# RWKV solve: steps two and three put on the off-diagonal quarters of the array, X and G computed in both halves

## The chip, the cores and the metric

One core of one Trainium2 chip runs the whole program. The metric is the device time of one execution in microseconds. The kernel before was run three times: 4854.69 us in the median, 4831.49 to 4855.27. The profiled execution is a further one.

## The reference, cut to what matters

The program is one inference step of a two-layer hybrid encoder trunk. Each layer projects its input, runs three branches (RWKV-7 time mixing, latent attention, stick-breaking attention) and merges them. The change touches the RWKV branch alone, whose recurrence for each head of width 64 is:

```python
def step(S, inp):
    r_t, w_t, k_t, v_t, kk_t, a_t = inp
    sa = jnp.einsum('bhij,bhj->bhi', S, -kk_t)
    S = (S * w_t[:, :, None, :] + sa[..., :, None] * (kk_t * a_t)[..., None, :]
         + v_t[..., :, None] * k_t[..., None, :])
    return S, jnp.einsum('bhij,bhj->bhi', S, r_t)
```

The kernel doesn't step through time. For each 64-row chunk it solves a triangular system: the recurrence inside a chunk is (I - A) z = rhs, with A strictly triangular. A's 16-row diagonal blocks are inverted by a product of powers (1, 2, 4, 8), and the blocks below them, four block rows deep, are taken in by three repeated steps q = G + X q. The results are the solved rows Z and a transposed W, which a later stage uses.

## The kernel before, in words

`rwkv` calls `rwkv_solve` once per pair of heads: 2 layers x 4 pairs, 8 calls. A call works through 9 tiles of 128 rows (`NT` = 9): tiles 0 to 7 (`NPT` = 8) are the prompt, two chunks of 64 rows each; tile 8 holds the sample sequences, whose chunks are so short that they need no repeated steps. All data are float32.

Every product is a matmul of a 64x64 weight. With `HALVES` the two chunks of a tile lie in partitions 0 to 63 and 64 to 127; chunk r reads partitions of half r and writes PSUM partitions of half r, so it uses the diagonal quarter (r, r) of the 128x128 array. The off-diagonal quarters (r, 1-r) are used by `scores` (all four) and by `akv` in tiles 0 to 7.

The work of one tile i on TensorE, by the values of k in `turn` (L658 to L701) and the other helpers:

- `scores(i)`: L608, L611. `rows(i)`: four 128x128 transposes, L620 to L623. `akv(i)`: L634.
- k = 0: first squaring `power(i, 0)` (L642, L648).
- k = 1: `power(i, 1)` and `inverse(i, 0)` (L655). k = 2: `power(i, 2)` (L644) and `inverse(i, 1)`. k = 3: `inverse(i, 2)`.
- k = 4: X and G (L682, L684), called xg below.
- k = 5, 6, 7: the three steps q = G + X q (L696), called step 5, 6, 7 below, as in the code; k = 8: the transpose of W (L701).

The order is written out by hand, per engine, and each engine works strictly through its own list with semaphore waits. TensorE interleaves tile i's k = 0 to 4 with the older tile i-1's k = 5 to 8:

```python
for i in range(NT + 1):
    turn(i, 0); turn(i - 1, 5); scores(i + 1)
    turn(i, 1); turn(i - 1, 6); akv(i)
    turn(i, 2); turn(i - 1, 7); turn(i, 3)
    rows(i + 1); turn(i - 1, 8); turn(i, 4)
```

(The kernel has one call a line.) ScalarE evacuates PSUM: `power` copies (L738), `akv` (L746), `w` (L765), `x_and_g` (L755), `rows` (L727 to L730). VectorE adds and masks in this order, which the change leaves alone: `solved(i-1, 5)` (q, L848), `mask(i+1, 0)` (L792), `inverse(i, 0)` (L826), `solved(i-1, 6)` (q, L848), `inverse(i, 1)`, `mask(i+1, 2)`, `mask(i+1, 3)`, `solved(i-1, 7)` (Z and W rows, L842 and L844), `inverse(i, 2)`, `mask(i+1, 4)`, `mask(i+1, 1)` (L803).

Of the kernel before, what the change touches and what calls it, by code (L numbers as in the profile page):

```python
# [8 lines left out]
ALU = mybir.AluOpType  # L9
# [4 lines left out]
P = 128  # L14
# [525 lines left out]
def rwkv_solve(nc, S, A, l, ps, con, T_, h, nx):  # L540
# [4 lines left out]
    RW, BK, vT, WS = T_.RW[h % 2], T_.BK, T_.vT, T_.WS  # L545
    TM, SI, SS, Z = T_.TM, T_.SI, T_.SS, T_.Z
    names = ("rows_ready", "rows_copied", "scores_ready", "sc_masked", "masked", "akv_ready", "akv_copied", "power_ready", "power_copied",
             "e_ready", "e_added", "xg_ready", "xg_copied", "q_ready", "q_added", "w_rows", "w_ready", "w_copied", "scores_read", "first_loaded", "vec", "act_own")
    with S.stage(*names) as (block, sb, (rows_ready, rows_copied, scores_ready, sc_masked, masked, akv_ready, akv_copied, power_ready, power_copied,
                                         e_ready, e_added, xg_ready, xg_copied, q_ready, q_added, w_rows, w_ready, w_copied, scores_read, first_loaded, vec, act_own)):  # L550
# [46 lines left out]
        def _(pe):  # L597
# [36 lines left out]
                        last = mm(ps[HALVES[r], akv_bank(i, r), 64 * hh:64 * hh + 64], KA[i % 2][cc, hh, :], TM[cc, i, 2, hc], start=True, stop=True)  # L634
                last.then_inc(akv_ready, 1)

            def power(i, n):
                for hh in range(2):
                    for r, rc in enumerate(HALVES):
                        m, mt = PW[n][i % 2][rc, hh, 0:64], PW[n][i % 2][rc, hh, 64:P]  # L640
                        if n < 2:
                            mm(step(i, r, P * hh, 64), mt, m, start=True, stop=True)  # L642
                        else:
                            last = mm(step(i, r, 64 * hh, 64), mt, m, start=True, stop=True)  # L644
                    for r, rc in enumerate(HALVES):
                        m, mt = PW[n][i % 2][rc, hh, 0:64], PW[n][i % 2][rc, hh, 64:P]
                        if n < 2:
                            last = mm(step(i, r, P * hh + 64, 64), m, mt, start=True, stop=True)  # L648
                last.then_inc(power_ready, 1)

            def inverse(i, k):
                for hh in range(2):
# [5 lines left out]
            def turn(i, k):  # L658
                if not 0 <= i < NT:
                    return  # L660
                if k == 0:
                    pe.wait_ge(masked, i + 1)
                    if i >= 2:
                        pe.wait_ge(w_copied, i - 1)
                    power(i, 0)
                elif k <= 2:
                    pe.wait_ge(power_copied, 3 * i + k)
                    power(i, k)
                    if k == 2:
                        pe.wait_ge(e_added, 3 * i + 1)  # L670
                    inverse(i, k - 1)
                elif k == 3:
                    pe.wait_ge(power_copied, 3 * i + 3)
                    pe.wait_ge(e_added, 3 * i + 2)
                    inverse(i, 2)
                elif k == 4:
                    pe.wait_ge(e_added, 3 * i + 3)
                    pe.wait_ge(akv_copied, i + 1)
                    for hh in range(2):
                        if i < NPT:  # L680
                            for r, rc in enumerate(HALVES):
                                mm(step(i, r, 64 * hh, 64), LO[i % 2][rc, hh, :], ET[i % 2][rc, hh, :], start=True, stop=True)  # L682
                        for r, rc in enumerate(HALVES):
                            last = mm(step(i, r, P + P * hh, P), ET[i % 2][rc, hh, :], RH[i % 2][rc, hh, :], start=True, stop=True)  # L684
                    last.then_inc(xg_ready, 1)
                elif k <= 7:
                    if i == NPT:
                        return
                    if k == 5:
                        pe.wait_ge(xg_copied, i + 1)  # L690
                    else:
                        pe.wait_ge(q_added, 2 * i + k - 5)
                    for hh in range(2):
                        for r, rc in enumerate(HALVES):
                            rhs = G[i % 2][rc, hh, :] if k == 5 else Q[rc, hh, :]
                            last = mm(out(i, r, k, P * hh, P), X[i % 2][rc, hh, :], rhs, start=True, stop=True)  # L696
                    last.then_inc(q_ready, 1)
                else:
                    pe.wait_ge(w_rows, i + 1)
                    pe.wait_ge(xg_copied, i + 1)  # L700
                    nc.tensor.transpose(ps[:, step_bank(i), 0:P], WP[i % 2][:, :], ident).then_inc(w_ready, 1)  # L701

            scores(0)
            rows(0)
            for i in range(NT + 1):
                turn(i, 0)
                turn(i - 1, 5)
                scores(i + 1)
                turn(i, 1)
                turn(i - 1, 6)  # L710
                akv(i)
                turn(i, 2)
                turn(i - 1, 7)
                turn(i, 3)
                rows(i + 1)
                turn(i - 1, 8)
                turn(i, 4)

        @block.scalar
        def _(act):  # L720
            copy = nc.scalar.activation

            def rows(i):
                if not 0 <= i < NT:
                    return
                act.wait_ge(rows_ready, i + 1)
                copy(RH[i % 2][:, :, 0:64], by_head(ps[:, 3, 0:P]), ACT.Copy)  # L727
                if i < NPT:
                    copy(TM[64:P, i, 3, :], ps[64:P, 3, 3 * P:4 * P], ACT.Copy)
                copy(TM[:, i, 0:3, :].rearrange("p q n -> p (q n)"), ps[:, 3, P:4 * P], ACT.Copy).then_inc(rows_copied, 1)  # L730

            def power(i, n):
                if not 0 <= i < NT:
                    return
                act.wait_ge(power_ready, 3 * i + n + 1)
                dst, w = (PW[n + 1][0], 2 * P) if n < 2 else (P8, P)
                for rc, bank in read_parts(i):
                    last = copy(dst[rc, :, :].rearrange("p h n -> p (h n)"), ps[rc, bank, 0:w], ACT.Copy)  # L738
                last.then_inc(power_copied, 1)

            def akv(i):
                if not 0 <= i < NT:
                    return
                act.wait_ge(akv_ready, i + 1)
                for rc, bank in akv_parts(i):
                    last = copy(RH[i % 2][rc, :, 64:P], by_head(ps[rc, bank, 0:P]), ACT.Copy)  # L746
                last.then_inc(akv_copied, 1)

            def x_and_g(i):
# [6 lines left out]
                last.then_inc(xg_copied, 1)  # L756

            def w(i):
                if not 0 <= i < NT:
                    return  # L760
                act.wait_ge(w_ready, i + 1)
                if i == NPT:
                    copy(WS[:, :], ps[:, step_bank(i), 0:P], ACT.Copy).then_inc(w_copied, 1)
                else:
                    copy(RW[:, i, 2:6:3, :], ps[:, step_bank(i), 0:P].rearrange("p (s n) -> p s n", s=2), ACT.Copy).then_inc(w_copied, 1)  # L765

            rows(0)
            for i in range(NT + 1):
                power(i, 0)
                power(i, 1)  # L770
                akv(i)
                power(i, 2)
                w(i - 1)
                x_and_g(i)
                rows(i + 1)

        @block.vector
        def _(dve):
# [50 lines left out]
            def solved(i, k):  # L829
# [3 lines left out]
                if i == NPT:  # L833
# [1923 lines left out]
```

## Time and profile before

| | |
|---|---|
| median of three runs | 4854.69 us |
| the profiled execution | 4857.2 us |
| its span, first to last instruction | 4855.6 us |
| mean granted TensorE clock | 0.96 |
| TensorE busy in the span | 4409.6 us (91%) |
| VectorE, ScalarE, GpSimd busy | 2218.3, 1625.0, 731.2 us |
| TensorE on L655, L642, L648, L696, L684 | 89.9, 82.4, 78.9, 80.6 + 41.9, 51.5 us |

"Busy" of TensorE counts a matmul from its start to its modelled end, and matmuls overlap, so a busy TensorE is not one that could take no more. The last row gives the solve's main groups. A timeline of one tile's turn says more about this stage than the shares do; such rows are given below. In them "xN" is the number of instruction records in the row (every float32 matmul here leaves two), the first number is the start in us from the span's start, and the second is the time from the first start to the last end.

### The profile page before, as it was taken

To read this page: it belongs to the slowest core of one execution; us is meant where nothing else is said; L and a number is where in the kernel's file an instruction comes from. 1 tells how busy PE (TensorE), PEld (TensorE's weight loads), DVE (VectorE), ACT (ScalarE), POOL (GpSimd) and SP (SyncE) were. 2 spreads that over 40 slices of the span, in tenths; PEclk is the share of its full clock that TensorE was granted. 3 is DMA by queue.
4 is the path that set the end of the run, shared out by engine and by line. 5 is a ranking of instruction groups with operands and counts; after the bars stand their busy time and mean duration, and the time that the engine had idled before them with its cause. 6 is when DMAs were issued, how large, how long until landed. Compare 5 with 4: busy or idle time off the path is not lost. (4 is left out here: it accounts for less than half of the span.)

```text
span 4855.6 us, 75921 instructions
## 1 busy us (share of the span) xinstructions
PE 4409.6 (91%) x29552; PEld 3049.7 (63%) x29552; DVE 2218.3 (46%) x4656; ACT 1625.0 (33%) x3862; POOL 731.2 (15%) x940
## 2 busy tenths in 40 slices
PE   5989897989889989999968999879898899899999
PEld 2656655657666667777436566656576666677774
DVE  2455655245524463434224555542455344535342
ACT  3324333345533342112033233333455334421110
POOL 0010010000001005543000100100000100155430
PEclk8999999999999999999989999989999999999999
DMA  5110110210021113232240101111100211223222
GB/s 223 27 17 26 25 28 24 74 51 20 16 73 63 56 46 107 94 105 74 75 185 22 33 10 25 28 40 58 51 20 16 82 54 56 73 84 110 88 78 69
DMA packets 152509, 292.71 MB, mean 60 GB/s; under 512 B 51769, under 2 KB 77625, under 8 KB 146818
## 3 DMA queue, kind: packets, MB, share of 16 engines
q1 hardware_dynamic: 152034, 283.07, 18.2%
q8 instruction: 238, 3.90, 0.3%
q10 hardware_dynamic: 112, 4.72, 0.3%
q14 instruction: 125, 1.02, 0.1%
HBM read 240.40 MB, written 52.06 MB: 60 GB/s over the span
## 5 line engine op out<-in xcount | busy, mean ns | idle before, releaser
L1041 PE MATMUL banks<-hT,w_piece 128*128 128x384 f32 x1536 | 550.8, 500 | 10.4 <-ACT raw L1145 10.2
L1041 PEld LDWEIGHTS banks<-hT,w_piece 128*128 128x128 f32 x1536 | 282.2, 195 | 181.3 <-issue 16.3
L2226 PE MATMUL banks<-hT,w_piece 128*128 128x384 f32 x1056 | 354.1, 489 | 1.5 <-ACT sb_gate_raw L2336 1.5
L2226 PEld LDWEIGHTS banks<-hT,w_piece 128*128 128x128 f32 x1056 | 196.1, 190 | 141.4 <-issue 16.6
L2577 PE MATMUL banks<-hT,mergedT 128*128 128x512 f32 x576 | 247.5, 592 | 0.0
L1992 DVE SCALAR_TENSOR_TENSOR keysT<-banks,gains,rstd 64x128 f32<-64x128 f32 (+1 forms) x272 | 112.1, 412 | 250.4 <-ACT rstd L1906 247.9
L2623 DVE TENSOR_TENSOR gate_quarters<-gate_kept,banks 128x288 f32<-128x288 f32 x144 | 65.4, 454 | 306.3 <-PE banks L2518 301.3
L2586 ACT ACTIVATE gate_kept<-banks 128x288 f32<-128x288 f32 x144 | 59.0, 410 | 434.8 <-PE banks L2518 434.8
L2577 PEld LDWEIGHTS banks<-hT,mergedT 128*128 128x128 f32 x576 | 109.4, 190 | 137.0 <-issue 136.8
L2398 DVE TENSOR_TENSOR_SCAN left<-pass,zero 128x384 f32<-128x384 f32 (+7 forms) x144 | 190.5, 1323 | 5.0
L2623 DVE TENSOR_TENSOR branch_quarters<-branch_kept,banks 128x288 f32<-128x288 f32 x144 | 65.4, 454 | 267.2 <-PE banks L2518 267.1
L2395 DVE TENSOR_TENSOR pass<-pass,constants 128x128 f32<-128x128 f32 x128 | 40.8, 319 | 312.1 <-ACT take L2347 309.5
L1002 POOL TENSOR_TENSOR state_decayed<-state,decay_of_chunk 128x128 f32<-128x128 f32 x120 | 85.9, 716 | 586.9 <-DVE state L1274 586.9
L1824 PE MATMUL banks<-keysT,queriesT 96*128 96x512 f32 (+3 forms) x384 | 151.9, 504 | 8.7 <-DVE queriesT L1992 8.7
L2518 PE MATMUL banks<-hT,w_gate_ahead 128*128 128x288 f32 x576 | 153.0, 417 | 7.4 <-PEq L132 7.4
L2518 PE MATMUL banks<-y_branch,w_branch 128*128 128x288 f32 x576 | 155.4, 406 | 0.0
L2518 PE MATMUL banks<-hT,w_gate 128*128 128x288 f32 x576 | 147.5, 406 | 0.0
L2518 PEld LDWEIGHTS banks<-hT,w_gate_ahead 128*128 128x128 f32 x576 | 112.3, 196 | 40.6 <-issue 8.8
L1922 ACT ACTIVATE exponentials<-banks,maximum 128x384 f32<-128x384 f32 (+4 forms) x144 | 104.1, 723 | 92.1 <-DVE maximum L2005 91.1
L2223 PE MATMUL banks<-w_piece,hT 128*128 128x128 f32 x1152 | 132.7, 276 | 0.0
L1933 ACT ACTIVATE exponentialsT<-banks 128x512 f32<-128x512 f32 (+3 forms) x208 | 94.9, 488 | 110.1 <-PE banks L1836 109.3
L2223 PEld LDWEIGHTS banks<-w_piece,hT 128*128 128x128 f32 x1152 | 130.2, 192 | 1.0
(393 smaller groups left out, 9476.2 us busy)
## 6 DMA issues: line engine op xcount, KB each, us to landing
w_piece<-in_w_cols SPq DMA_DIRECT2D x66, 512.0 KB, 4.4
w_ada<-in_w_ada SPq DMA_DIRECT2D x24, 1024.0 KB, 9.6
w_gate_ahead<-in_w_cols SPq DMA_DIRECT2D x48, 512.0 KB, 4.2
w_branch<-in_w_br SPq DMA_DIRECT2D x96, 256.0 KB, 2.8
w_gate<-in_w_cols SPq DMA_DIRECT2D x48, 512.0 KB, 4.2
y_branch<-y_gated SPq DMA_DIRECT2D x12, 1152.0 KB, 8.5
sb_cached_keysT<-in_sbkT SPq DMA_DIRECT2D x8, 1024.0 KB, 7.3
sb_cached_values<-in_sbv SPq DMA_DIRECT2D x8, 1024.0 KB, 5.2
```

The lines of the kernel that those rows point to most:

```text
L1002: G.tensor_tensor(SD[:, :], ST[:, :], R.pend[h % 2][:, n + 1:n + 2].broadcast_to([P, P]), ALU.mult).then_inc(sd_made, 1)
L1041: last = mm(dst, w[0 if kind in ("k", "v") else 1][:, k, :], hT[:, k, c], start=(k == 0), stop=(k == KD - 1))
L1824: last = mm(ps[:, b0 + a // 512, 0:e - a], Q[hh][:, P * i:P * i + P], K[hh][:, a:e], start=True, stop=True)
L1922: do(E[u % 3][:, 0:width(u)], sbank(u)[:, 0:width(u)], ACT.Exp, bias=mx[:, u:u + 1], scale=scale, accum_out=rsum[:, u:u + 1]).then_inc(exp ...
L1933: do(ET[:, s % 4, units[u][3], 0:cnt, :].rearrange("p q n -> p (q n)"), ps[:, ring_bank(("t", u, g)), 0:P * cnt], Copy).then_inc(ring_free, 1)
L1992: ins = V.scalar_tensor_tensor(to[hh][0:64, c], ps[hc, bank[n], at], par[hc, gain:gain + 1], rs[x % 2][hc, at], ALU.mult, ALU.mult)
L2223: last = mm(ps[:, bank[n], P * q:P * q + P], hT[:, k, P * i:P * i + P], w_of[wn][:, k, :], start=(k == 0), stop=(k == KD - 1))
L2226: last = mm(ps[:, bank[n], 0:TG], w_of[wn][:, k, :], hT[:, k, TG * g:TG * g + TG], start=(k == 0), stop=(k == KD - 1))
L2398: own(V.tensor_tensor_scan(mine[:, 0:n][:, ::-1], G[k][:, 0:n][:, ::-1], zero[:, 0:1].broadcast_to([P, n]), 1.0, ALU.mult, ALU.add))
L2518: ins = mm(ps[:, bank, 0:TQ], w[:, k, :], b[:, k, :], start=(first and k == 0), stop=(k == half - 1), skip_group_check=True)
L2577: last = mm(ps[:, banks[j % 4], :], M[:, k, P * i:P * i + P], w_half(n)[:, k, :], start=(k == 0), stop=(k == KD - 1))
L2623: own(V.tensor_tensor(dst, src, ps[:, bank, 0:TQ], ALU.add), added)
```

## The change

Steps 6 and 7 of tile i-1 run on the off-diagonal quarters, interleaved instruction by instruction with powers 2 and 4 of tile i. For that X and G are also computed with their halves swapped, into PSUM bank 2, and copied by a new ScalarE copy `swapped` to a new tile. Step 6 takes X from its own half and leaves its result in the other; its sum uses the swapped G; step 7 takes the swapped X and comes back. ScalarE's `rows(i + 1)` is moved ahead of `w` and `x_and_g`. VectorE's order stays.

```diff
+        SW = sb("x_and_g_swapped", [P, 3 * P])
...
+        XS, GS = SW[:, 0:P].rearrange("p (h n) -> p h n", h=2), SW[:, P:3 * P].rearrange("p (h n) -> p h n", h=2)
...
-            def power(i, n):
-                for hh in range(2):
-                    for r, rc in enumerate(HALVES):
...
+            def square(i, n, hh, r, transposed):
+                m, mt = PW[n][i % 2][HALVES[r], hh, 0:64], PW[n][i % 2][HALVES[r], hh, 64:P]
+                if transposed:
+                    return mm(step(i, r, P * hh + 64, 64), m, mt, start=True, stop=True)
+                return mm(step(i, r, (P if n < 2 else 64) * hh, 64), mt, m, start=True, stop=True)
+
+            def across(i, k, hh, r):
+                if not 0 <= i < NPT:
+                    return None
+                lhsT, rhs = (X[i % 2], Q) if k == 6 else (XS, Q)
+                return mm(out(i, 1 - r, k, P * hh, P), lhsT[HALVES[r], hh, :], rhs[HALVES[r], hh, :], start=True, stop=True)
...
+            def powers_and_step(i, n):
+                stepped = 0 <= i - 1 < NPT
+                if stepped:
+                    pe.wait_ge(q_added, 2 * (i - 1) + n)
+                    if n == 2:
+                        pe.wait_ge(swap_copied, i)
+                if i < NT:
+                    pe.wait_ge(power_copied, 3 * i + n)
+                for hh in range(2):
+                    for r in range(2):
+                        if i < NT:
+                            power = square(i, n, hh, r, 0)
+                        turned = across(i - 1, n + 5, hh, r)
+                    if i < NT and n < 2:
+                        for r in range(2):
+                            power = square(i, n, hh, r, 1)
+                if stepped:
+                    turned.then_inc(q_ready, 1)
+                if i < NT:
+                    power.then_inc(power_ready, 1)
+                    if n == 2:
                         pe.wait_ge(e_added, 3 * i + 1)
-                    inverse(i, k - 1)
...
+                    inverse(i, n - 1)
...
+            def x_and_g(i):
+                if i >= NT:
+                    return
+                pe.wait_ge(e_added, 3 * i + 3)
+                pe.wait_ge(akv_copied, i + 1)
+                if 1 <= i < NPT:
+                    pe.wait_ge(swap_copied, i)
+                for hh in range(2):
+                    for r, rc in enumerate(HALVES):
                         if i < NPT:
...
+                            mm(step(i, r, 64 * hh, 64), LO[i % 2][rc, hh, :], ET[i % 2][rc, hh, :], start=True, stop=True)
+                            mm(ps[HALVES[1 - r], 2, 64 * hh:64 * hh + 64], LO[i % 2][rc, hh, :], ET[i % 2][rc, hh, :], start=True, stop=True)
+                    for r, rc in enumerate(HALVES):
+                        last = mm(step(i, r, P + P * hh, P), ET[i % 2][rc, hh, :], RH[i % 2][rc, hh, :], start=True, stop=True)
+                        if i < NPT:
+                            last = mm(ps[HALVES[1 - r], 2, P + P * hh:2 * P + P * hh], ET[i % 2][rc, hh, :], RH[i % 2][rc, hh, :], start=True, stop=True)
+                last.then_inc(xg_ready, 1)
...
             for i in range(NT + 1):
-                turn(i, 0)
-                turn(i - 1, 5)
+                first_power(i)
+                first_step(i - 1)
                 scores(i + 1)
-                turn(i, 1)
-                turn(i - 1, 6)
+                powers_and_step(i, 1)
                 akv(i)
-                turn(i, 2)
-                turn(i - 1, 7)
-                turn(i, 3)
+                powers_and_step(i, 2)
+                last_inverse(i)
                 rows(i + 1)
-                turn(i - 1, 8)
-                turn(i, 4)
+                turn_w(i - 1)
+                x_and_g(i)
...
+            def swapped(i):
+                if not 0 <= i < NPT:
+                    return
+                act.wait_ge(xg_ready, i + 1)
+                if i >= 1:
+                    act.wait_ge(q_ready, 3 * i)
+                    act.wait_ge(q_added, 2 * i)
+                copy(SW[:, :], ps[:, 2, 0:3 * P], ACT.Copy).then_inc(swap_copied, 1)
+
...
                 power(i, 0)
+                swapped(i - 1)
                 power(i, 1)
                 akv(i)
                 power(i, 2)
+                rows(i + 1)
                 w(i - 1)
                 x_and_g(i)
-                rows(i + 1)
...
                 dve.wait_ge(q_ready, 3 * i + k - 4)
+                if k == 6:
+                    dve.wait_ge(swap_copied, i + 1)
...
-                        ins = V.tensor_tensor(Q[rc, :, :], g[rc, :, :], by_head(q), ALU.add)
+                        ins = V.tensor_tensor(Q[rc, :, :], (g if k == 5 else GS)[rc, :, :], by_head(q), ALU.add)
```

`first_power`, `first_step`, `last_inverse` and `turn_w` hold the same matmuls and waits as `turn` with k = 0, 5, 3 and 8.

## Rows read from the trace of the kernel before

**Rows 1.** Windows: length, then busy us of each engine, clock, DMA.

```profile
195.05:245.05 50.00, 46.93 (x1087) 40.48 (x1082) 32.61 (x106) 22.36 (x72) 0.00 (x0) 1.00 0.03 9
3652.20:3655.60 3.40, 1.82 (x14) 1.59 (x14) 2.30 (x9) 1.89 (x6) 0.00 (x0) 1.00 0.16 58
```

**Rows 2.** Timeline of TensorE's matmuls in one turn: start, length, instruction.

```profile
214.36 0.54 PE L696 MATMUL banks<-x_and_g 64*64 64x128 f32 x5
...
214.80 0.55 PE L608 MATMUL banks<-a_r_and_w,k_and_b 64*64 64x128 f32 x12
...
215.59 0.33 PE L642 MATMUL banks<-power 64*64 64x64 f32 x4
...
216.10 0.40 PE L655 MATMUL banks<-inverseT,power 64*64 64x64 f32 x8
216.34 0.28 PE L696 MATMUL banks<-q,x_and_g 64*64 64x128 f32 x2
216.35 0.27 PE L634 MATMUL banks<-bk_and_vu_rows,scores_ka 64*64 64x64 f32 x2
...
216.67 0.28 PE L696 MATMUL banks<-q,x_and_g 64*64 64x128 f32 x2
216.78 0.42 PE L644 MATMUL banks<-power 64*64 64x64 f32 x8
217.04 0.40 PE L655 MATMUL banks<-inverseT,power 64*64 64x64 f32 x8
217.54 0.65 PE L696 MATMUL banks<-q,x_and_g 64*64 64x128 f32 x8
218.02 0.41 PE L655 MATMUL banks<-inverseT,power 64*64 64x64 f32 x8
...
218.75 0.27 PE L623 MATMUL banks<-constants,k_and_b 128*128 128x128 f32 x1
...
219.13 0.33 PE L682 MATMUL banks<-inverseT,off_diagonal 64*64 64x64 f32 x4
```

**Rows 3.** Timeline of VectorE in the same turn.

```profile
215.06 0.42 DVE L848 TENSOR_TENSOR q<-x_and_g,banks 128x256 f32<-128x256 f32 x1 [0.69 <-PE banks L696]
...
216.62 0.29 DVE L826 TENSOR_TENSOR inverseT<-inverseT,banks 128x128 f32<-128x128 f32 x1 [0.63 <-PE banks L655]
217.06 0.42 DVE L848 TENSOR_TENSOR q<-x_and_g,banks 128x256 f32<-128x256 f32 x1 [0.15 <-PE banks L696]
217.55 0.29 DVE L826 TENSOR_TENSOR inverseT<-inverseT,banks 128x128 f32<-128x128 f32 x1
...
218.79 0.29 DVE L826 TENSOR_TENSOR inverseT<-inverseT,banks 128x128 f32<-128x128 f32 x1
```

**Rows 4.** Timeline of ScalarE in the same turn and to the next.

```profile
213.82 0.49 ACT L755 ACTIVATE x_and_g<-banks 128x384 f32<-128x384 f32 x1 [0.76 <-PE banks L684]
214.21 0.27 ACT L727 ACTIVATE rhs<-banks 128x128 f32<-128x128 f32 x1
214.49 0.27 ACT L729 ACTIVATE bk_and_vu_rows<-banks 64x128 f32<-64x128 f32 x1
...
215.16 0.38 ACT L738 ACTIVATE power<-banks 128x256 f32<-128x256 f32 x1
...
220.07 0.49 ACT L755 ACTIVATE x_and_g<-banks 128x384 f32<-128x384 f32 x1 [0.61 <-PE banks L684]
```

**Rows 5.** Timeline of TensorE in a call's last turn, `akv` on the diagonal.

```profile
240.90 0.60 PE L696 MATMUL banks<-q,x_and_g 64*64 64x128 f32 x8
241.33 0.40 PE L634 MATMUL banks<-bk_and_vu_rows,scores_ka 64*64 64x64 f32 x8
```

**Rows 6.** Timeline of ScalarE, start and end of that last turn.

```profile
238.78 0.49 ACT L755 ACTIVATE x_and_g<-banks 128x384 f32<-128x384 f32 x1 [0.59 <-PE banks L684]
...
244.43 0.38 ACT L755 ACTIVATE x_and_g<-banks 128x256 f32<-128x256 f32 x1 [0.38 <-PE banks L684]
```

More of the change, by code:

```diff
@@ L656, in inverse, with first_power @@
                 last.then_inc(e_ready, 1)
-            def turn(i, k):
-                if not 0 <= i < NT:
+            def first_power(i):
+                if i >= NT:
                     return
[L661 to L669, printed above, removed]
-                        pe.wait_ge(e_added, 3 * i + 1)
-                    inverse(i, k - 1)
[L672 to L679, printed above, removed]
-                        if i < NPT:
[L681 to L701, printed above, removed]
@@ new lines, in first_power, with first_step @@
+                pe.wait_ge(masked, i + 1)
+                if i >= 2:
+                    pe.wait_ge(w_copied, i - 1)
+                for hh in range(2):
+                    for transposed in range(2):
+                        for r in range(2):
+                            last = square(i, 0, hh, r, transposed)
+                last.then_inc(power_ready, 1)
+            def first_step(i):
+                if not 0 <= i < NPT:
+                    return
+                pe.wait_ge(xg_copied, i + 1)
+                for hh in range(2):
+                    for r, rc in enumerate(HALVES):
+                        last = mm(out(i, r, 5, P * hh, P), X[i % 2][rc, hh, :], G[i % 2][rc, hh, :], start=True, stop=True)
+                last.then_inc(q_ready, 1)
@@ new lines, in powers_and_step @@
+            def powers_and_step(i, n):
[6 more added lines that the diff above has]
+                    pe.wait_ge(power_copied, 3 * i + n)
+                for hh in range(2):
+                    for r in range(2):
[3 more added lines that the diff above has]
+                    if i < NT and n < 2:
+                        for r in range(2):
+                            power = square(i, n, hh, r, 1)
[4 more added lines that the diff above has]
+                    if n == 2:
+                        pe.wait_ge(e_added, 3 * i + 1)
+                    inverse(i, n - 1)
@@ new lines, in last_inverse @@
+            def last_inverse(i):
+                if i >= NT:
+                    return
+                pe.wait_ge(power_copied, 3 * i + 3)
+                pe.wait_ge(e_added, 3 * i + 2)
+                inverse(i, 2)
+            def x_and_g(i):
+                if i >= NT:
+                    return
+                pe.wait_ge(e_added, 3 * i + 3)
+                pe.wait_ge(akv_copied, i + 1)
+                if 1 <= i < NPT:
+                    pe.wait_ge(swap_copied, i)
+                for hh in range(2):
+                    for r, rc in enumerate(HALVES):
+                        if i < NPT:
+                            mm(step(i, r, 64 * hh, 64), LO[i % 2][rc, hh, :], ET[i % 2][rc, hh, :], start=True, stop=True)
+                            mm(ps[HALVES[1 - r], 2, 64 * hh:64 * hh + 64], LO[i % 2][rc, hh, :], ET[i % 2][rc, hh, :], start=True, stop=True)
+                    for r, rc in enumerate(HALVES):
+                        last = mm(step(i, r, P + P * hh, P), ET[i % 2][rc, hh, :], RH[i % 2][rc, hh, :], start=True, stop=True)
+                        if i < NPT:
+                            last = mm(ps[HALVES[1 - r], 2, P + P * hh:2 * P + P * hh], ET[i % 2][rc, hh, :], RH[i % 2][rc, hh, :], start=True, stop=True)
+                last.then_inc(xg_ready, 1)
@@ L703, in _, with turn_w @@
+            def turn_w(i):
+                if i < 0:
+                    return
+                pe.wait_ge(w_rows, i + 1)
+                pe.wait_ge(xg_copied, i + 1)
+                nc.tensor.transpose(ps[:, step_bank(i), 0:P], WP[i % 2][:, :], ident).then_inc(w_ready, 1)
             scores(0)
@@ L756, in x_and_g @@
                 last.then_inc(xg_copied, 1)
+            def swapped(i):
+                if not 0 <= i < NPT:
+                    return
+                act.wait_ge(xg_ready, i + 1)
[3 more added lines that the diff above has]
+                copy(SW[:, :], ps[:, 2, 0:3 * P], ACT.Copy).then_inc(swap_copied, 1)
             def w(i):
```

14 lines of the change are left out of this document (2 added, 12 removed).

## The prediction

> **What bounds the solve now.** I read the granted clock and busy time of a stretch first, then the timelines of the three working engines through one turn, from one xg copy on ScalarE to the next. Over 50 us of the first call TensorE is busy 46.93 us at the full clock of 2.4 GHz [rows 1]. That looks like a TensorE bound, and it isn't one: that time counts each matmul to its modelled end, and those ends overlap. The turn has to be followed from release to release. It is 6.25 us long (213.82 to 220.07) [rows 4]; the last turn of a call is 5.65 us (238.78 to 244.43) [rows 6]. There are 8 turns in each of 8 calls, 64 in all: 64 x 6.2 = about 400 us of 4857 that the change can touch.
>
> I count from the xg copy, called a0 (213.82). Step 5 starts at a0+0.54 and its sum q on VectorE runs from a0+1.24 to a0+1.66 [rows 2, 3]. ScalarE, after xg, first does the `rows` copies and only then the power copy (a0+1.34 to 1.72), and that releases power 1 at a0+1.77 (215.59) [rows 2, 4]. From there: inverse 0 at +0.51 after power 1, its sum on VectorE at +1.03; the sum of step 6 at +1.47; power 2 at +1.19, inverse 1 at +1.45; step 7 at +1.95, 0.06 after the end of step 6's sum [rows 2, 3]. VectorE works in its written order, so the sum of inverse 1 (217.55) waits for step 6's sum (end 217.48), though its own matmuls, 217.04 + 0.40, were done. The reader should see in these rows that **two chains share VectorE**: the powers with the inverse, and the steps. From the sum of inverse 1 the end of the turn is fixed: 1.24 us of VectorE work (two masks, Z, W rows) to the sum of inverse 2 at 218.79, 0.34 to xg at 219.13, 0.94 to the next xg copy at 220.07 [rows 2 to 4]. So what matters is when the sum of inverse 1 starts: a0+3.73 now. 3.73 + 1.24 + 0.34 + 0.94 = 6.25.
>
> **The change, part by part.**
>
> Do the quarters work side by side? `akv` is issued after step 6. In ordinary tiles it is on the off-diagonal quarters and its first matmuls start at 216.35, with step 6's first at 216.34, while step 6's last start at 216.67 [rows 2]. In a call's last tile `akv` is on the diagonal and starts at 241.33, 0.43 after step 6's 240.90 [rows 5]. So a step costs 0.43 on its own quarters and nothing on the others. Scores use all four quarters: 12 records of 128 columns take 0.55 us, 0.27 of it the last one's length, so they start 25 ns apart; the 8 of step 7 alone take 0.65, with 0.28 for the last, 53 ns apart [rows 2]. I take the off-diagonal work as free of array time.
>
> Block one, power 1 with step 6. The block now waits for the sum of step 5, ending a0+1.66, plus 0.06: it starts at **a0+1.72** instead of a0+1.77. Behind the waiting block stand inverse 0 and `akv`. The power copy is no longer behind `rows` (the move) and is ready earlier, at about a0+0.39 + 0.38 + 0.05 = a0+0.82, so the new wait is the later one. Gain 0.05. Power 1 keeps its diagonal quarters 0.51 us, in which step 6 (0.43) runs beside it.
>
> VectorE's turn comes next, and here the gain is lost. Inverse 0 is still issued behind power 1, so its sum starts at +1.03 and ends at +1.32. The sum of step 6 is written behind it on VectorE: it starts, with 0.04 between dependent sums, at +1.36 although its matmuls were done at about 0.7, and ends at +1.78. Before it started at +1.47. Moving step 6 0.75 us forward has brought its sum forward by only 0.11.
>
> Block two, power 2 with step 7, now waits for that sum: it starts at 1.72 + 1.78 + 0.06 = **a0+3.56**. Step 7 is 0.16 earlier than before (a0+3.72), but power 2, which used to start at a0+2.96 as soon as its copy was there, is 0.60 later, and inverse 1 stands behind it. Inverse 1 at +0.26 (its distance behind power 2 now), its sum 0.51 after (217.04 to 217.55, of which 0.40 + 0.11 are its own latency, as for inverse 0: 216.10 to 216.62): a0 + 3.56 + 0.77 = **a0+4.33**, where it was a0+3.73. Step 7's matmuls end 0.65 after their start, a0+4.21, so Z and W rows, behind two masks, are not late. Inverse 2 needs the sum's end, a0+4.62 + 0.06 = 4.68, and its own sum could go at 5.20; VectorE is free at 4.33 + 1.24 = 5.57. So the tail of 1.24 + 0.34 + 0.94 stays and each turn is **+0.60 us**.
>
> In the last turn the next tile's masks and `rows` are absent, so the tail is shorter, but the same wait for step 6's sum stands ahead of inverse 1. I take 0.60 there too, an estimate for 8 turns of the 64; between 0.3 and 0.7 it moves the sum by 2 us at most.
>
> X and G twice: 8 more matmuls a tile, on the other quarters beside the old ones. At the rate of scores, 25 ns a record, its 16 records of 128 columns take 0.40 us and the 16 of 64 columns, at half of that, 0.20: 0.60, where the 8 and 8 of now at 53 and 27 take 0.64. So nothing; if they didn't overlap at all, 0.64 a turn. I take 0, since scores are the nearest row.
>
> The new copy `swapped`, 0.49 (the length of its twin L755 [rows 4]), comes after the power copy, a0+0.8 to 1.3. ScalarE's next is the copy of power 1 at about a0+2.45. It is covered; without that cover it would be 0.4 (its pitch) a turn. Its data are wanted at a0+3.1 first. `rows` on ScalarE moved before `w` and xg: the transposes are ready 1.00 after the start of inverse 2 (218.02 to 218.75 + 0.27 [rows 2]), at a0+5.68, plus 0.04; three copies have a pitch of 0.95 (214.21 to 215.16), `w` 0.28 at most (214.21 to 214.49) [rows 4], so xg can be copied at a0+6.95 against 6.85 ready. Between 0 and 0.10; I take 0.05, in 56 turns (the last turn of a call has no `rows`).
>
> Sum: 64 x 0.60 = 38.4, 56 x 0.05 = 2.8, together **+41 us**. On the profiled execution (4857.2) that is 4898.4; the median is 2.5 below it, so I forecast **4896 us**.
>
> A rule weighed against the rows: the Trainium skill, "TensorE: Matmul & The Clock Gate", section "Part 3: Packing small matmuls — row/col tiling", says that MATMULs keep program order in start and end and only weight loads are pulled ahead. By that rule `akv` could not start at 216.35, before step 6's remaining starts up to 216.67 [rows 2]; the trace disagrees. What such an order would give is the second rival.
>
> **The rivals.**
>
> *Faster, because TensorE is what binds.* Then what leaves the diagonal quarters counts: step 6, 0.44 (216.34 to 216.78), and step 7, 0.48 (217.54 to 218.02) [rows 2], 0.92 x 64 = 59 us, 4796. The busy share [rows 1] speaks for it. It decides the time only if power 2 starts no later than now, that is if the sum of step 6 ended by about a0+2.9; VectorE's order puts it at 3.50. Chance 4%.
>
> *Slower by more: starts in program order.* If a step's third and fourth matmul must start before what is issued behind them, power 2 and inverse 1 are stretched by the step: inverse 1 at +0.43 to 0.46 after block two instead of 0.26. +0.2 x 64 = 13 us, 4909. For it: power and step are now interleaved one by one. Against it: [rows 2, 5]. Chance 20%.
>
> *No change that shows.* If the sum of step 6 were not held behind inverse 0 (say its sum comes out when its own matmuls end, a0+2.45 to 2.87), block two would start at a0+2.93 and inverse 1's sum at a0+3.70, a parity: 4855. VectorE's list speaks against it. Together with partial covers that eat half of the sum: chance 10%.
>
> *The change doesn't do what it says:* off-diagonal work not free. xg twice is +0.6 and the steps in the powers' way another 0.4: 64 x 1.0 = 64 us more, 4960. Scores and `akv` [rows 2, 5] speak against it. Chance 4%.
>
> *The clock falls within the solve,* since TensorE now idles about 0.9 us before block two in each turn. A stretch with 1.82 us busy of 3.40 kept the full clock [rows 1], and the solve keeps about three quarters busy. Chance 2%; at 1.2 GHz the 400 us would grow by a quarter or more, over 4950.
>
> **How the numbers follow.** The forecast has 60%, with its own range of 4884 to 4908 (ScalarE 0 to 0.10 a turn, 0.1 us either way in the turn). I widen to the in-order case above and to part-covers and a differently placed clock fall between stages (the three runs are 24 us apart) below: 4872 to 4916. A difference of 0.5%, 24 us, is about what a measurement of this kernel can tell from none. Slower by more than that: forecast, in-order case, the last two, less the forecast's low tail: 0.85. Within: 0.11. Faster: 0.04.
>
> **What would show it.** The turn between xg copies at 6.85 to 6.95; TensorE idle about 0.9 us ahead of power 2 (L644's successor), released by the sum q on VectorE, not by the power copy; the sum of step 6 starting within 0.05 of the end of inverse 0's; `swapped` never a releaser; `akv`, power 2 and inverse 1 starting while the step beside them still has starts to come. A turn under 6.4, or power 2 starting about 1.2 after power 1, would prove me wrong; a turn of 7.05 with inverse 1 0.45 behind power 2 would show the order rule; a longer xg to first power would show quarters that collide.

## The result and the profile after

The changed kernel takes 4928.35 us in the median (4925.7 to 4934.3, four runs) against 4853.91 us: a ratio of 1.0159, 95% interval 1.0138 to 1.0181. It is slower by 74 us. The forecast was 4896 us, 41 us slower, with a range up to 4916: the side was right, the size was not. The traces are 77.1 us apart (4932.7 against 4855.6). From the first to the last xg copy of a call passes 49.4 to 49.7 us before and 57.8 to 58.8 after, 68.8 us over the eight calls. The other 8.3 us lie outside the solves.

The page of the changed kernel: line, engine, instruction, count, then busy us, mean ns, and TensorE's idle time ahead of these instructions with what ended it.

```profile
L643 PE MATMUL banks<-power 64*64 64x64 f32 x1728 | 121.3, 238 | 77.9 <-DVE q L890 57.0
L655 PE MATMUL banks<-inverseT,power 64*64 64x64 f32 x1728 | 92.9, 224 | 47.3 <-DVE inverseT L866 47.3
```

L643 is the squaring in the three powers, L655 the matmuls of the inverse. TensorE now idles 57.0 us before it for the sum q, 0.89 in each of 64 turns, as forecast (0.9). Before, TensorE's idle time ahead of L655 was 4.8 us in all. The windows of the changed kernel (as in [rows 1]) say the same: over the same 50 us TensorE is busy 37.86 us, not 46.93, and the clock isn't full throughout.

```profile
195.05:245.05 50.00, 37.86 (x1051) 32.62 (x1043) 28.70 (x95) 20.89 (x66) 0.00 (x0) 0.93 0.01 3
```

Now one usual turn of the changed kernel, to be held against [rows 2 to 4]. ScalarE first:

```profile
222.31 0.49 ACT L760 ACTIVATE bk_and_vu_rows<-banks 128x384 f32<-128x384 f32 x1
222.70 0.27 ACT L804 ACTIVATE a_r_and_w<-banks 128x128 f32<-128x128 f32 x1
222.86 0.50 ACT L785 ACTIVATE x_and_g<-banks 128x384 f32<-128x384 f32 x1
223.84 0.38 ACT L768 ACTIVATE power<-banks 128x256 f32<-128x256 f32 x1 [0.48 <-PE banks L642]
224.12 0.49 ACT L795 ACTIVATE x_and_g_swapped<-banks 128x384 f32<-128x384 f32 x1
225.54 0.38 ACT L768 ACTIVATE power<-banks 128x256 f32<-128x256 f32 x1 [0.93 <-PE banks L642]
...
227.29 0.28 ACT L768 ACTIVATE power<-banks 128x128 f32<-128x128 f32 x1 [1.20 <-PE banks L643]
...
230.12 0.50 ACT L785 ACTIVATE x_and_g<-banks 128x384 f32<-128x384 f32 x1
```

VectorE in the same turn:

```profile
224.28 0.42 DVE L890 TENSOR_TENSOR q<-x_and_g,banks 128x256 f32<-128x256 f32 x1 [0.98 <-PE banks L676]
...
225.78 0.29 DVE L866 TENSOR_TENSOR inverseT<-inverseT,banks 128x128 f32<-128x128 f32 x1 [0.60 <-PE banks L655]
226.10 0.42 DVE L890 TENSOR_TENSOR q<-x_and_g_swapped,banks 128x256 f32<-128x256 f32 x1
227.49 0.29 DVE L866 TENSOR_TENSOR inverseT<-inverseT,banks 128x128 f32<-128x128 f32 x1 [0.97 <-PE banks L655]
...
228.73 0.29 DVE L866 TENSOR_TENSOR inverseT<-inverseT,banks 128x128 f32<-128x128 f32 x1
```

TensorE in the same turn:

```profile
221.81 0.27 PE L720 MATMUL banks<-inverseT,off_diagonal 64*64 64x64 f32 x1
...
223.12 0.33 PE L643 MATMUL banks<-power 64*64 64x64 f32 x4 [0.41 <-ACT a_r_and_w L804]
...
223.60 0.49 PE L676 MATMUL banks<-x_and_g 64*64 64x128 f32 x5
...
224.75 0.27 PE L643 MATMUL banks<-power 64*64 64x64 f32 x1
...
226.58 0.27 PE L643 MATMUL banks<-power 64*64 64x64 f32 x1 [0.85 <-DVE q L890]
...
226.80 0.23 PE L643 MATMUL banks<-power 64*64 64x64 f32 x2
...
226.86 0.22 PE L655 MATMUL banks<-inverseT,power 64*64 64x64 f32 x1
...
226.97 0.28 PE L649 MATMUL banks<-q,x_and_g_swapped 64*64 64x128 f32 x2
226.98 0.29 PE L655 MATMUL banks<-inverseT,power 64*64 64x64 f32 x4
227.93 0.45 PE L655 MATMUL banks<-inverseT,power 64*64 64x64 f32 x8 [0.66 <-DVE inverseT L866]
...
229.07 0.27 PE L720 MATMUL banks<-inverseT,off_diagonal 64*64 64x64 f32 x1
```

The reader is to see three things. Power 2 (226.58) starts on the end of step 6's sum (226.10 + 0.42), which started when inverse 0's sum (225.78 + 0.29) was done; the power's own copy had ended at 225.54 + 0.38, 0.60 before the sum did. The first power of this turn (223.12) waited for W's copy (222.70 + 0.27), 1.31 after xg's start at 221.81, where it was 0.72. And inverse 1's sum (227.49) comes 0.22 after its matmuls' modelled end (226.98 + 0.29), where it was 0.11. The turn in four pieces, cut as the prediction cuts it:

| us | xg copy to power 1 | to inverse 1's sum | to inverse 2's sum | to next xg copy | turn |
|---|---|---|---|---|---|
| before | 1.77 | 1.96 | 1.24 | 1.28 | 6.25 |
| forecast | 1.72 | 2.61 | 1.24 | 1.33 | 6.90 |
| after | 1.89 | 2.74 | 1.24 | 1.39 | 7.26 |

### The profile page after: what moved, and what is told of

Same layout as the page of the kernel before. It is cut to its first block and busy times, and to the rows that moved or that the text cites. A ratio compares the mean times of both kernels' runs of the same rounds, so it can differ in the third digit from the quotient of the medians.

```text
span 4932.7 us, 78217 instructions
## 1 busy us (share of the span) xinstructions
PE 4391.1 (89%) x30576; PEld 3019.8 (61%) x30576; DVE 2213.9 (45%) x4656; ACT 1652.4 (33%) x3926; POOL 731.8 (15%) x940
## 5 line engine op out<-in xcount | busy, mean ns | idle before, releaser
L643 PE MATMUL banks<-power 64*64 64x64 f32 x1728 | 121.3, 238 | 77.9 <-DVE q L890 57.0
L643 PEld LDWEIGHTS banks<-power 64*64 64x64 f32 x1728 | 90.4, 142 | 108.8 <-DVE q L890 67.7
L768 ACT ACTIVATE power<-banks 128x256 f32<-128x256 f32 (+1 forms) x216 | 75.2, 348 | 184.1 <-PE banks L642 105.5
L655 PE MATMUL banks<-inverseT,power 64*64 64x64 f32 x1728 | 92.9, 224 | 47.3 <-DVE inverseT L866 47.3
```

The costliest lines, as they stand in the source:

```text
L643: return mm(step(i, r, (P if n < 2 else 64) * hh, 64), mt, m, start=True, stop=True)
```

## The experiments

Each ran beside the kernel before on the same chip; the ratio to it is given with its 95% interval. The chip was not the same for all experiments, so where times of different experiments are compared, the ratios or the distances to the kernel before are taken. The pieces of a turn are read in the third call's third turn.

**Rows copies back in their place (e1).**

```diff
                 power(i, 2)
-                rows(i + 1)
                 w(i - 1)
                 x_and_g(i)
+                rows(i + 1)
```

> Changed kernel, with ScalarE's rows(i+1) back behind w and x_and_g; nothing else. Theory: the move put the copy of W behind three rows copies, and the first power of the next tile waits for that copy (215.86 in the changed kernel, 1.16 after xg's start, where it was 0.72), and step 5 stands behind it on TensorE. Undone, xg to its copy is 0.94 again instead of up to 1.12 and xg copy to power 1 is 1.77 instead of 1.83: the usual turn 7.26 becomes 7.0 to 7.05, in 56 turns 12 to 14 us, about 4915. Rival, the prediction's term for the move (0.05 a turn): 3 us, 4925. Second rival, the move also helps by letting the power copy go early: no change or slower.

Measured: 4926.66 us, 1.0138 (1.0121 to 1.0155). The usual turn is 7.15. ScalarE and TensorE of this kernel:

```profile
573.57 0.49 ACT L785 ACTIVATE x_and_g<-banks 128x384 f32<-128x384 f32 x1 [0.65 <-PE banks L725]
...
574.91 0.38 ACT L768 ACTIVATE power<-banks 128x256 f32<-128x256 f32 x1
```

```profile
574.11 0.54 PE L676 MATMUL banks<-x_and_g 64*64 64x128 f32 x5 [0.15 <-ACT x_and_g L785]
...
575.43 0.24 PE L643 MATMUL banks<-power 64*64 64x64 f32 x1
```

Both things that I wanted undone are undone: step 5 starts 0.54 after the xg copy, not 0.74, and xg is copied 0.08 sooner. But power 1 starts at +1.86, hardly before the +1.89 of the changed kernel: the power copy is behind `rows` again and ends at +1.72. So the move has a gain (the power copy is early) and a price (W's copy, and with it the next tile's first power, step 5 and its sum, are late), and they nearly cancel. My expectation took the price alone as theory and left the gain to a rival, though both count: 0.11 a turn, not 0.21 to 0.26. In the time it can't be told from nothing.

**No wait in front of the power (e2).**

```diff
-                if stepped:
-                    pe.wait_ge(q_added, 2 * (i - 1) + n)
-                    if n == 2:
-                        pe.wait_ge(swap_copied, i)
+                if stepped and n == 1:
+                    pe.wait_ge(q_added, 2 * (i - 1) + n)
...
+                if stepped and n == 2:
+                    pe.wait_ge(q_added, 2 * (i - 1) + n)
+                    pe.wait_ge(swap_copied, i)
+                    for hh in range(2):
+                        for r in range(2):
+                            turned = across(i - 1, n + 5, hh, r)
+                    turned.then_inc(q_ready, 1)
```

> Changed kernel, with power 4's squaring and inverse 1 issued as soon as their own inputs are there; step 7 stays on the off-diagonal quarters but is issued behind them, with the wait for step 6's sum in front of it alone. Theory: the loss is that wait in front of the power. The power starts 1.19 after power 1 again instead of 1.82, inverse 1's sum starts 1.97 after power 1 instead of 2.74; the turn 7.26 becomes about 6.5, 48 us over 64 turns, about 4880. Rival (the loss is in computing X and G twice, in quarters that collide or in the clock): 4920 or more.

Measured: 4874.07 us, 1.0034 (1.0021 to 1.0047); turn 6.54. TensorE of this kernel:

```profile
565.55 0.27 PE L643 MATMUL banks<-power 64*64 64x64 f32 x1
...
566.77 0.45 PE L643 MATMUL banks<-power 64*64 64x64 f32 x8 [0.24 <-ACT power L774]
567.05 0.40 PE L655 MATMUL banks<-inverseT,power 64*64 64x64 f32 x8
567.38 0.65 PE L649 MATMUL banks<-q,x_and_g_swapped 64*64 64x128 f32 x8
```

Power 2 is released by its own copy again, 1.22 after power 1, and step 7 follows on its own quarters beside inverse 1. This one edit takes the ratio from 1.0159 to 1.0034, about four fifths of the loss: 15 us over the kernel before are left of 74. The theory holds, in mechanism and size; X and G are still computed twice. But the edit does two things: it takes the wait away from the power, and it takes step 7's matmuls out from among the power's. The next experiment does the second alone and has a turn of 7.14; the wait by itself is the difference to it, 7.14 - 6.54 = 0.60 a turn, the forecast's own term (37 us by the medians, of the same chip).

**Same waits, step 7 issued last (e3).** The waits stay at the head of block two; the four squarings and the four matmuls of inverse 1 are issued ahead of step 7's four instead of among them.

```diff
-                        turned = across(i - 1, n + 5, hh, r)
+                        if n == 1:
+                            turned = across(i - 1, n + 5, hh, r)
...
                     inverse(i, n - 1)
+                if stepped and n == 2:
+                    for hh in range(2):
+                        for r in range(2):
+                            turned = across(i - 1, n + 5, hh, r)
+                    turned.then_inc(q_ready, 1)
```

> Changed kernel, block two with the same waits at its head, but the four matmuls of the power and the four of inverse 1 are issued first and step 7 behind them. Theory (a matmul group's signal waits for what was issued before it, although starts overlap): inverse 1's sum, now 0.92 after the block's start, comes at 0.77 as in the kernel before; the turn 7.26 becomes 7.11, 9 to 10 us, about 4918; the power copy comes 0.55 after the block's start instead of 0.71. Rival (step 7 slows the neighbours because both read the same partitions): sum stays at 0.9, no change.

Measured: 4911.18 us, 1.0106 (1.0087 to 1.0124); turn 7.14. TensorE, and then ScalarE and VectorE behind it:

```profile
578.37 0.45 PE L643 MATMUL banks<-power 64*64 64x64 f32 x8 [0.85 <-DVE q L896]
578.65 0.22 PE L655 MATMUL banks<-inverseT,power 64*64 64x64 f32 x2
```

```profile
578.86 0.28 ACT L774 ACTIVATE power<-banks 128x128 f32<-128x128 f32 x1 [0.99 <-PE banks L643]
```

```profile
579.16 0.29 DVE L872 TENSOR_TENSOR inverseT<-inverseT,banks 128x128 f32<-128x128 f32 x1 [0.85 <-PE banks L655]
```

The power copy comes 0.49 after the block's start and inverse 1's sum 0.79, against 0.71 and 0.91 in the changed kernel (226.58 to 227.29 and 227.49). The turn is shorter by the same 0.12, so that is what step 7 in between cost. It is 8 us over 64 turns; the solves of this trace are 14.6 us shorter than the changed kernel's (450.3 against 464.9), and the clock falls of the changed kernel, described below, are absent from them. The rest of the difference in time lies outside the solves. In the changed kernel the power's last matmuls (the row at 226.80, two records) have their modelled end at 227.03, and ScalarE is released only at 227.29, with the end of step 7 (226.97 + 0.28 = 227.25). The trace also records when the semaphores were raised: the power's at 227.26, step 7's at 227.31 and inverse 1's at 227.40, which is the order in which they were issued, and in e3, with step 7 issued last, the power's at 578.84, inverse 1's at 579.07 and step 7's at 579.34. Starts overtake one another across quarters, signals do not. That speaks against the expectation's rival too, a step that slows its neighbours by reading the same partitions: the power's last matmul starts about 0.23 behind its first in the changed kernel and in e3 alike, so the matmuls were not slowed, their signal was held.

The trace of the kernel before had the sign of it. There `akv` is issued behind step 6; its matmuls end by the model at 216.79, and its copy starts only at 217.08, after step 6's end (216.67 + 0.28 = 216.95 in [rows 2]):

```profile
216.57 0.22 PE L634 MATMUL banks<-bk_and_vu_rows,scores_ka 64*64 64x64 f32 x2
```

```profile
217.08 0.28 ACT L746 ACTIVATE rhs<-banks 128x128 f32<-128x128 f32 x1 [0.38 <-PE banks L634]
```

The Trainium skill's rule in "TensorE: Matmul & The Clock Gate", section "Part 3: Packing small matmuls — row/col tiling", that matmuls keep order in start and end, is by these rows wrong for the starts; for the ends the signals agree with it (the ends in the rows are modelled and settle nothing).

**VectorE takes step 6's sum first (e4).**

```diff
-                inverse(i, 0)
                 solved(i - 1, 6)
+                inverse(i, 0)
                 inverse(i, 1)
```

> Changed kernel, with VectorE taking step 6's sum before inverse 0's; nothing else. Theory (step 6's matmuls are done early, at 0.7 after power 1, and only VectorE's order holds its sum to 1.35): the sum starts at about 0.75, block two starts 1.23 after power 1 instead of 1.82, inverse 1's sum 2.2 after power 1 instead of 2.74: turn 7.26 becomes about 6.7, 35 us, about 4893. Rival (step 6 isn't early, the off-diagonal matmuls are late themselves): the sum starts at 1.2 or later and the turn stays above 7.1.

Measured: 4886.69 us, 1.0063 (1.0045 to 1.0081); turn 6.74. VectorE of this kernel, whose power 1 starts at 557.00:

```profile
557.78 0.42 DVE L890 TENSOR_TENSOR q<-x_and_g_swapped,banks 128x256 f32<-128x256 f32 x1 [0.34 <-PE banks L649]
558.24 0.29 DVE L866 TENSOR_TENSOR inverseT<-inverseT,banks 128x128 f32<-128x128 f32 x1
559.23 0.29 DVE L866 TENSOR_TENSOR inverseT<-inverseT,banks 128x128 f32<-128x128 f32 x1 [0.70 <-PE banks L655]
```

The sum starts 0.78 after power 1 instead of 1.35: the off-diagonal matmuls were done, VectorE's order held the sum. Exchanging two lines takes the ratio to 1.0063, more than half of the loss: 28 us over the kernel before are left of 74.

**X and G twice in the kernel before (e7).** The 8 extra matmuls and the copy `swapped` are those of the change's diff; nothing reads the copy, and steps 5 to 7 stay as before.

> Kernel before, with X and G computed a second time on the off-diagonal quarters into bank 2 and copied by ScalarE behind the first power copy, as in the changed kernel; the copy is read by nothing. It prices the doubling by itself. Theory: the quarters work side by side and the copy falls into ScalarE's idle time; xg start to its copy is 0.97 instead of 0.94, the turn 6.25 becomes 6.25 to 6.35, under 6 us, 4855 to 4865. Rival (the doubling holds a good part of the loss): 0.3 to 0.64 a turn, 4875 to 4900.

Measured: 4860.79 us, 1.0007 (0.9995 to 1.0020); turn 6.28. The doubling costs 0.03 a turn, 2 us over the 64 turns; the time itself can't be told from that of the kernel before.

**Both undone (e9)**: e2 and e1 together.

> Changed kernel with both undone, the wait for step 6's sum in front of the power and the move of ScalarE's rows; steps on the off-diagonal quarters, step 6 interleaved with power 2 and the doubling stay. It closes the account. Theory: from the turn of the kernel with the first undone (6.54) the move gives 0.1 back, as it did when undone alone (7.26 to 7.15): 6.43, and what is left over the kernel before (6.25) is the doubling's 0.03 and power 1 about 0.1 later behind its wait for step 5's sum; some 4864 to 4872. Rival (the two undone overlap, one hides the other): 6.5 or more, or 6.3 or less.

Measured: 4862.63 us, 1.0013 (1.0002 to 1.0025); turn 6.43, as expected, and the time just under the 4864 to 4872 expected. Its pieces are 1.86, 2.02, 1.24 and 1.31. Against the kernel before, 0.03 is the doubling, 0.09 power 1 and 0.06 the longer way to inverse 1's sum. Why power 1 starts 0.14 after the end of the power copy (0.05 before), with the sum of step 5 already there, I didn't find.

**Rows copies behind the first power copy, in the kernel before (e5).** If the power copy's place matters, it can be had without the change:

```diff
                 power(i, 0)
+                if i:
+                    rows(i)
                 power(i, 1)
                 akv(i)
                 power(i, 2)
                 w(i - 1)
                 x_and_g(i)
-                rows(i + 1)
```

> Kernel before, with ScalarE's rows copies of tile i behind the first power copy of tile i, where they stand neither before the power copy nor before W and xg; TensorE and VectorE as before. Theory: power 1 starts when scores leave the array, about 1.6 after the xg copy instead of 1.77; turn 6.25 becomes about 6.1, 8 to 11 us less, about 4845. Rival (TensorE's queue is full): no change.

Measured: 4829.95 us, 0.9948 (0.9931 to 0.9965), **faster than both kernels**; turn 6.01. TensorE and ScalarE of this kernel:

```profile
543.22 0.38 PE L611 MATMUL banks<-k_and_b,a_r_and_w 64*64 64x64 f32 x5
543.43 0.28 PE L642 MATMUL banks<-power 64*64 64x64 f32 x4
```

```profile
541.85 0.49 ACT L755 ACTIVATE x_and_g<-banks 128x384 f32<-128x384 f32 x1 [0.61 <-PE banks L684]
...
547.86 0.49 ACT L755 ACTIVATE x_and_g<-banks 128x384 f32<-128x384 f32 x1 [0.61 <-PE banks L684]
```

Power 1 starts 1.58 after the xg copy, right behind scores, instead of 1.77. The mechanism is the expected one, but the gain is over twice the 8 to 11 us expected: the turn is 0.24 shorter instead of 0.15, and that is 16 us over the solves (380.1 of the span against 396.1). The two traces are 31 us apart, the medians 28; what is not in the solves lies in stages whose code is the same (see below).

**Masks early as well (e6).** Two lines of VectorE's list are moved up, `mask(i + 1, 2)` and `mask(i + 1, 3)`, to behind `mask(i + 1, 0)`.

> As the last kernel, and VectorE takes the next tile's masks 2 and 3 before inverse 0's sum instead of after inverse 1's. Theory: Z and W rows wait for step 7 and not for the masks, so inverse 2's sum moves by 0.05 at most; turn about 6.05 to 6.1, under 3 us from the last kernel. Rival (VectorE's 1.24 us of work behind inverse 1's sum is what binds): 0.3 to 0.4 a turn less, 20 us.

Measured: 4830.24 us, 0.9957 (0.9937 to 0.9976); turn 6.05. No gain: Z and W rows wait for step 7 in this order, not for the masks, as VectorE's row shows:

```profile
549.05 0.29 DVE L843 TENSOR_TENSOR z_solved<-x_and_g,banks 128x128 f32<-128x128 f32 x1 [0.45 <-PE banks L696]
```

**Off-diagonal steps that stand before no power (e8).** TensorE issues power and inverse, then the step with its wait; ScalarE and VectorE as in e6, with `swapped` behind `rows`.

```diff
-                powers_and_step(i, 1)
+                power_and_inverse(i, 1)
+                step_across(i - 1, 1)
                 akv(i)
-                powers_and_step(i, 2)
+                power_and_inverse(i, 2)
+                step_across(i - 1, 2)
```

> Changed kernel, steps 6 and 7 on the off-diagonal quarters, but in TensorE's old order: power and inverse first, the step behind them with its wait; ScalarE and VectorE ordered as in the last kernel. Theory: with no step in front of a power the quarters bring their small gain. Power 1 at about 1.7, inverse 1's sum 1.97 later, Z and W rows earlier by 0.1, turn about 6.1: 4840 to 4850, level with the kernel that only moves the rows copies. Rival (off-diagonal steps are worth something once the waits are gone): turn 5.9 or less, 4835.

Measured: 4838.96 us, 0.9965 (0.9953 to 0.9977); turn 6.00, 0.05 under e6's and level with e5's. That is what the off-diagonal quarters are worth here, the doubling included; in the time it doesn't show (e6 and e5 are 9 us faster by the medians, from stages outside the solves).

**The change's own TensorE order with its partners fitted to it (e10)**: VectorE takes masks 2 and 3, then step 6's sum, then inverse 0's; ScalarE's `rows(i)` stands behind the first power copy.

> Changed kernel with TensorE's order and waits as they are, steps interleaved with the powers; VectorE takes step 6's sum before inverse 0's and the next tile's masks before both, ScalarE's rows stand behind the first power copy. Theory: TensorE's interleaving was not wrong in itself, its partners' order was; power 2 starts 1.3 after power 1, inverse 1's sum 2.2 after it, inverse 2's sum 0.9 after that instead of 1.23: turn 6.15 to 6.25, 4840 to 4860, level with before and behind the kernel before with rows moved (6.01). Rival (the wait in front of the power costs in any order): 6.5 or more, 4870.

Measured: 4873.42 us, 1.0037 (1.0021 to 1.0052); turn 6.47, next to the rival's 6.5. Power 1 starts 1.72 after the xg copy, the forecast's own figure for the wait on step 5's sum. But the pieces behind it are 2.27, 0.99 and 1.49 (2.2, 0.9 and 1.3 expected). VectorE of this kernel:

```profile
563.11 0.29 DVE L867 TENSOR_TENSOR inverseT<-inverseT,banks 128x128 f32<-128x128 f32 x1 [0.65 <-PE banks L655]
563.43 0.29 DVE L885 TENSOR_TENSOR z_solved<-x_and_g,banks 128x128 f32<-128x128 f32 x1
563.64 0.28 DVE L887 TENSOR_TENSOR w_rows<-x_and_g,banks 128x128 f32<-128x128 f32 x1
564.10 0.29 DVE L867 TENSOR_TENSOR inverseT<-inverseT,banks 128x128 f32<-128x128 f32 x1 [0.18 <-PE banks L655]
```

Inverse 2's sum now waits for TensorE (0.18 idle), not for VectorE. Even with its partners fitted in this way, the step in front of the power costs 0.47 a turn over e8, which also doubles X and G and uses the off-diagonal quarters (and whose VectorE takes inverse 0's sum before step 6's). Other orders of VectorE's list were not tried.

## Why the prediction was wrong, point by point

- **Off-diagonal work is free of array time: right.** e7 prices the doubling at 0.03 a turn (forecast 0), and e8 runs both steps there without harm.
- **The new wait in front of power 2: right, and the main term.** Power 2 comes 1.83 after power 1 (forecast 1.84); e2 without the wait and e4 with an earlier sum take back most of the loss, and e2 against e3 prices the wait at the forecast's 0.60.
- **The wait for step 5's sum, gain 0.05: wrong, a loss of 0.12.** Power 1 starts at +1.89, not +1.72, 0.05 behind the sum's end as forecast; but the sum itself starts at +1.42, where I had kept +1.24. I had charged the move of `rows` to the xg copy alone. Behind `rows` stands W's copy as well, and the next tile's first power waits for it (`w_copied`, 223.12), with step 5 queued behind that power on TensorE. I did not follow the moved copies to that wait, though it stands in the kernel, in `turn` with k = 0: 0.17 a turn. e10, with `rows` moved behind the first power copy instead, has the sum at +1.24 and power 1 at +1.72. e1 alone doesn't show it: its sum is at +1.24 too, but there power 1 waits for the power copy.
- **Inverse 1's sum 0.77 after block two: wrong, 0.91.** The second rival (starts in program order, +0.2, given 20%) is near it in size, but its mechanism is not what happened: inverse 1 starts 0.28 after block two, not 0.43. The starts are not in order, as [rows 2, 5] had it, but the signals wait for what was issued between: e3, 0.12 a turn.
- **ScalarE's copy of xg 0 to 0.10 late, taken as 0.05: 0.11.** Xg to its copy went from 0.94 to 1.05; 0.03 of it is the doubling (e7 has 1.31 from inverse 2's sum where before has 1.28).
- **The last turn +0.60: measured +0.84.** In the first call's last turn power 1 starts 1.72 after the xg copy, on step 5's sum, where it was 1.37: the new wait, a gain of 0.05 in the forecast, costs 0.35 there. Inverse 1's sum is 2.74 behind power 1 instead of 2.17, and the rest of the turn is 0.08 shorter.
- **The clock stays full in the solve (fall given 2%): wrong.** Each call of the changed kernel has a fall between its turns, the kernel before has none. Windows of the changed kernel, 6 us and then 3.4 us of the third call:

```profile
592.20:598.20 6.00, 4.22 (x125) 3.82 (x125) 3.14 (x12) 2.11 (x7) 0.00 (x0) 1.00 0.01 3
598.20:601.60 3.40, 3.40 (x65) 3.10 (x67) 1.59 (x5) 2.38 (x7) 0.00 (x0) 0.50 0.02 5
```

  The clock fell to its lower level, 1.2 GHz, after a stretch with TensorE busy 4.22 of 6.00 us. The two turns around it took 7.88 and 7.54 instead of 7.26 each: about 0.9 us a call, some 7 us in all. [Rows 1] showed one stretch busy 1.82 of 3.40 at the full clock; one such row does not exclude a fall, and it was cut from denser work: over 3640 to 3665 us TensorE is busy 22.10 of 25.00.

Added up: 0.17 + 0.13 + 0.06 = 0.36 a turn over the forecast's 0.65, about 20 us over 56 turns (a little less, since a call's first and seventh turns grew by under 1.01), 2 us from the last turns and some 7 us of clock account for the solves (68.8 against 41.2 us); 8.3 us lie outside them.

Those 8.3 us, and the 15 us that e5 gains outside them, are in stages with unchanged code. The stage behind the second call, from its last xg copy to the next call's first, before and after:

```profile
421.17:542.24 121.07, 108.24 (x534) 65.58 (x536) 67.32 (x144) 36.95 (x86) 17.90 (x17) 0.94 0.16 33
```

```profile
436.22:563.37 127.15, 114.41 (x554) 68.64 (x556) 67.40 (x144) 37.89 (x89) 17.89 (x17) 0.89 0.13 32
```

The columns are those of [rows 1]. This stretch is 6.1 us longer at a mean clock of 0.89 instead of 0.94, with VectorE and GpSimd as busy as before. The mean clock of the whole execution goes the same way: 0.955 after, 0.960 before, 0.964 in e5 and e6, 0.960 in e8, whose solves are as short as e5's and which is 9 us slower. But that pair is one of seven, and others go the other way: the stretch behind the first call takes 127.03 before and 126.16 after. The stretch behind the second takes 118.4 (e5) to 127.1 us in the twelve traces, the longer the lower its clock, and e7's trace has 14 us more outside the solves than the trace before, though its median is only 3 us above the kernel before. One trace of each kernel can't tell 8.3 us there from such scatter. For e5 and e6 the medians stand 28 and 27 us under the kernel before where the solves give 16 and 14, so something outside them is likely real. How a shorter or longer solve moves the clock's falls in the stages behind it is not settled; nothing here varied it alone.

## What to carry to other kernels

Before two pieces of work are merged into one block on an engine, list what each waits for: the merged block starts at the later of the two, and everything queued behind the earlier one pays. Here the sum q came 0.6 us after the power copy, because another engine's list had a different piece in front of it, and free array quarters could not make up for that. And when an instruction is moved past others, follow each of the instructions that it now delays to whoever waits for it; the cheapest gain of the study (e5, 28 us below before, 16 of them in the solves) was three copies moved to where nobody stood behind them.

## What the hardware showed that I had not expected

Between quarters of the array these float32 matmuls start out of the order in which they were issued (226.86 of inverse 1 before 226.97 of step 7), but their signals come in that order (227.26, 227.31, 227.40): four matmuls of a step among the power's delayed ScalarE's release from 0.49 to 0.71 after the block's start and the inverse's sum from 0.79 to 0.91. The clock also fell inside a stage in which TensorE was busy 70% of the time (4.22 of 6.00 us in the third call), and it did so in every call. It did so in e1 too (turn 7.15) and not in e3 (turn 7.14), which differ in the order of `rows` and of step 7 and not in length, so the length of the turn alone doesn't decide it; what does is open.
